# Second block of a two-block network: stages that end and begin by blocks of 128 tokens, with norms, transposes and router products block by block

## The chip, the cores and the metric

The kernel is written in Bass and runs on one core of one Trainium2 chip. The metric is the device time of one execution in microseconds. All data are float32. [...] A product (`mm`) of float32 shows as two records of MATMUL, each with a weight load of its own (LDWEIGHTS, on the row PEld); a transposition shows as one record.

## The reference, cut to what matters

x is 256 tokens by 1024 channels. Two networks follow each other, each of two layers. The first (attention and FFN) ends with an FFN of squared relus and an RMS norm:

```python
        ff = jnp.square(jax.nn.relu(jnp.einsum('bsd,df->bsf', h2, w_ff1[l])))
        x = x + jnp.einsum('bsf,fd->bsd', ff, w_ff2[l])
    return _rms_norm(x, final_g)
```

The second is modulated by a condition c:

```python
    for l in range(DEPTH):
        mod = cond @ ada_w[l] + ada_b[l]
        shift_m, scale_m, gate_m, shift_f, scale_f, gate_f = mods
        h = rms_norm(x, mix_norm_g[l]) * (1.0 + scale_m) + shift_m
        proj = h @ w_in[l]          # pooling, convolution and spatial gating parts
        ...
        x = x + gate_m * (mixed @ w_out[l])
        h = rms_norm(x, ffn_norm_g[l]) * (1.0 + scale_f) + shift_f
        # layer 0: y = swiglu(h), width 2816; layer 1: top 2 of 8 experts, width 3584
        x = x + gate_f * y
    return rms_norm(x, final_norm_g)
```

## The kernel before, in words

The engines' programs are written out by hand, in order, and meet at semaphores. The order of the work on an engine is the order of its program. x lies as [128 tokens, 2 blocks b, 1024]; hT is its normalised transpose, 8 tiles k of [128 channels, 256 tokens]. PSUM has eight banks: G0 to G3, T0, T1, S0, S1; H4 is the list S0, S1, T0, T1. A result of 256 tokens by 1024 columns fills the four G banks: bank j = 2*half + b holds columns of half `half` for the tokens of block b, and is called a quarter.

**Turn of a stage in the second block.** When a stage's last product is done, TensorE computes the gate sums (L2095, two products of 512 columns with a matrix of ones, into T1 and S1) and ScalarE copies them (L937) for a later gating. VectorE's `add_gated` waits for all four banks, multiplies each by the gate row (L1110) and adds it to x (L1114); ScalarE squares and sums block by block (L728); POOL's `norm_root` waits for both blocks and takes the root (L634, L635); VectorE scales both blocks (`normalise`, L1075); TensorE's `turn` waits for both, transposes them in four pairs into T0 and T1 (L1746), two tiles k over 256 tokens at a time, and ScalarE (L745) and VectorE (L1088) evacuate them with scale and shift into hT. Then TensorE starts the next stage. At the end of the first block there is a second norm in the chain: VectorE multiplies x by the final gain (L1443), ScalarE squares that too (L929), POOL takes two roots (L673 to L679) and L1446 scales by both.

**Mixer.** `features(0)`, `features(1)` (L2121, 24 products of 256 columns each) make the convolution's inputs, `tokens(2)` (L2113, 8 products of 256 columns for each block) the pooling's, `tokens(3)` and `tokens(4)` the gating unit's. VectorE makes the gated input, runs nine taps of the convolution (L1474, L1477) and then copies the two pooling banks (L1485, L1487), for which `tokens(3)` waits. At the end `product(k)` runs all four quarters for one tile k of the mixed channels; the last three tiles come from the convolution and are waited for one by one.

**FFN of layer 0.** Eleven steps of 256 hidden columns: `ffn_step` makes gate and up products (L2215, 4 x 8 products of 256 columns), then the down products of the step (L2221, 2 hidden tiles x 4 quarters of 512 columns) onto the G banks, which a product with zeros opens (L1756) and another closes (L1760). The weights lie in two slots of 3 MB that overlap the slots of the mixer's weights, so the second mixer's weights (L585) are asked for when both are free.

**Expert stage of layer 1.** Router products (L2233), selection, gather (L2247), then per expert 14 steps with five weight slots of 3 MB, filled from SyncE's queue (L573). POOL releases the first two slots behind `norm_root(U_FFN + 2)`, the other three behind the copies of the gate rows (L937).

**First block's FFN.** Eight chunks: up products in four tiles (L2047), ScalarE's relu (L918), VectorE's square (L1420), down products (L2054). The last chunk's second half of down products runs by quarters. In layer 1 ScalarE takes the sigmoid of the condition (L911) before the first relu; it waits for the condition and for the gate bias, which POOL asks for after the norm's root. VectorE and ScalarE do the modulation's products (`ada`, `row_sums`) between the chunks, with weights that POOL's queue brings (L651).

Of the kernel before, what the change touches and what calls it, by code (L numbers as in the profile page):

```python
# [9 lines left out]
ALU = mybir.AluOpType  # L10
# [3 lines left out]
P = 128  # L14
# [75 lines left out]
QUARTERS = ((0, 1, 2, 3), (0, 2, 1, 3))  # L90
ROW_L1 = 2 * KD + KCQ + KCKV
# [53 lines left out]
def build(nc, t):  # L145
    ctx = ExitStack()
    with ctx:
# [157 lines left out]
        rstd_ok = sig("rstd_ok", 1)  # L305
# [57 lines left out]
        w2_mm = sig("w2_mm", 7)  # L363
# [79 lines left out]
        def used_at(l, pos):  # L443

            return l * (L1_CHUNKS // NSLOT) + pos // NSLOT + 2

# [166 lines left out]
        def _(pool):  # L613
# [15 lines left out]
            def inv_root(v, out, count, u_wait, done):  # L629
# [5 lines left out]
                pool.tensor_tensor(out, v, mhalf[:, 0:n], ALU.pow).then_inc(done.sem, 1)  # L635

            def norm_root(u):
                pool.wait_ge(ss_ok.sem, ss_ok.at(u, 2))
                inv_root(small[:, 0:2], small[:, 2:4], None, u, rstd_ok)
# [13 lines left out]
            for l in range(DEPTH):  # L653
# [4 lines left out]
                inv_root(small[:, 8:28], small[:, 32:52], A_DIM, l, ars_ok)  # L658
# [6 lines left out]
                inv_root(small[:, 64:80], small[:, 80:96], 2 * B_DIM, l, subrs_ok)  # L665
# [6 lines left out]
            pool.wait_ge(ss_ok.sem, ss_ok.at(U_MIX, 2))  # L672
            step.do(pool.tensor_tensor(small[:, 0:2], small[:, 0:2], epsc[:, 0:2], ALU.add))  # L673
            step.do(pool.tensor_tensor(small[:, 2:4], small[:, 0:2], mhalf[:, 0:2], ALU.pow))
            step.do(pool.tensor_tensor(small[:, 6:8], small[:, 2:4], small[:, 2:4], ALU.mult))
            pool.wait_ge(ssq_ok.sem, 2)
            step.do(pool.tensor_tensor(small[:, 4:6], small[:, 4:6], small[:, 6:8], ALU.mult))
            step.do(pool.tensor_tensor(small[:, 4:6], small[:, 4:6], epsc[:, 0:2], ALU.add))
            pool.tensor_tensor(small[:, 304:306], small[:, 4:6], mhalf[:, 0:2], ALU.pow).then_inc(rstd_ok.sem, 1)  # L679
# [8 lines left out]
            for l in range(DEPTH):  # L688
                if l:
                    norm_root(U_MIX + 2 * l)  # L690
# [5 lines left out]
                norm_root(U_FFN + 2 * l)  # L696
# [21 lines left out]
        def _(act):  # L718
# [6 lines left out]
            def square_rows(u, b):  # L725

                act.wait_ge(x_new.sem, added(u, b))
                act.activation(squares[:, b, :], x[:, b, :], ACT.Square, scale=D ** -0.5, accum_out=small[:, b:b + 1]).then_inc(ss_ok.sem, 1)  # L728
# [44 lines left out]
            for l in range(DEPTH):  # L773
# [7 lines left out]
                act.wait_ge(rstd_ok.sem, rstd_ok.at(l * 2, 1))  # L781
# [127 lines left out]
                if l == DEPTH - 1:  # L909
                    act.wait_ge(ada_bias.sem, 32)  # L910
                    act.activation(condsig, condrow, ACT.Sigmoid).then_inc(cond_ok.sem, 1)  # L911
                for c in range(8):
# [6 lines left out]
                    if l == DEPTH - 1:  # L919
                        for n in ADA_SLOTS[0][c]:  # L920
                            row_sums(0, n)

            for l in range(DEPTH):
                u = U_MIX + 2 * l
                norm_squares(u)
                if l == 0:
                    for b in range(NB):
                        act.wait_ge(scaled_ok.sem, b + 1)
                        act.activation((pT, o)[b][:, :, :].rearrange("p i n -> p (i n)"), scaled[:, b, :], ACT.Square, scale=D ** -0.5, accum_out=small[:, 4 + b:5 + b]).then_inc(ssq_ok.sem, 1)  # L929
                def gate_rows(g):  # L930

                    for n, bank in ((1, T[1]), (0, S[1])):
# [5 lines left out]

                gate_rows(0)
                act.wait_ge(mulc_ok.sem, mulc_ok.at(l, 1))  # L940
                turned_evac(u, xn_turned, hT_act, mulc[:, l, 0], mods[:, l, 0:KD])

                for c in range(KCONV):
                    if c < 2:
                        act.wait_ge(w2_mm.sem, w2_mm.at(l, 3 + c))
# [24 lines left out]
                norm_squares(u + 1)  # L970
# [1556 lines left out]
```

## Time and profile before

| | |
|---|---|
| median of 3 runs | 2643.82 us (2643.2 to 2645.14) |
| profiled execution | 2643.71 us, its span 2641.7 us |
| granted TensorE clock, mean | 0.975 |
| TensorE busy | 2463.8 us, 93% |
| VectorE, ScalarE, POOL busy | 25%, 16%, 2% |
| DMA | 617.36 MB, mean 234 GB/s |

Busy matmul time is modelled and not a measure of peak; what counts here is where TensorE stands and what released it. In a timeline a row gives start, length, engine, line, operation, output<-input, shapes, count, and in brackets the idle time before it with its releaser.

### The profile page before, as it was taken

What the parts mean: (1) busy time and instruction counts of PE and PEld (TensorE: products, weight loads), DVE (VectorE), ACT (ScalarE), POOL (GpSimd) and SP (SyncE); (2) the same over time, 40 slices, a digit from 0 to 9 for tenths busy, and PEclk for the clock granted to TensorE, in tenths of its full rate; (3) what the DMA queues carried; (4) which work ended last, traced back from release to release, by engine and by line L of the source; (5) the groups of instructions that cost most, each with busy time, mean ns of one, the idle gap of its engine ahead of it and who ended that gap; (6) DMA issues with size and microseconds to landing.
All of it is one profiled execution on the core that took longest, in us unless ns stands there. A gap on an engine that the chain in (4) does not pass through costs nothing.

```text
span 2641.7 us, 27045 instructions
## 1 busy us (share of the span) xinstructions
PE 2463.8 (93%) x11010; PEld 1548.3 (59%) x11011; DVE 648.9 (25%) x1428; ACT 412.9 (16%) x1035; POOL 50.6 (2%) x96
## 2 busy tenths in 40 slices
PE   8999999999999999898998979888999889979997
PEld 5566566656664666656776744448984444434443
DVE  0453200013532244262343531111011101010101
ACT  1242000012430223101231010111001101000101
POOL 0000000000000000000000000000000000000000
PEclk9999999999999999999999989998998999999999
DMA  6323444333233777334774349995755999768971
GB/s 240 123 96 120 148 159 146 142 139 130 96 120 135 299 299 270 114 118 188 295 297 195 109 180 427 420 430 227 281 240 250 429 432 374 305 262 373 390 291 59
DMA packets 62540, 617.36 MB, mean 234 GB/s; under 512 B 4144, under 2 KB 4272, under 8 KB 36832
## 3 DMA queue, kind: packets, MB, share of 16 engines
q1 hardware_dynamic: 57488, 558.38, 52.9%
q0 software_dynamic: 4656, 56.47, 5.4%
q8 instruction: 89, 1.46, 0.2%
q10 hardware_dynamic: 288, 0.90, 0.1%
q14 instruction: 19, 0.16, 0.0%
HBM read 614.69 MB, written 1.05 MB: 233 GB/s over the span
## 4 chain that ended last, share of the span: by engine, by line
PE 82%; DMA 9%; DVE 3%; issue 3%; ACT 1%; POOL 1%; ACTq 0%; DVEq 0%; SPq 0%; POOLq 0%
DMA big<-in_moe_pack 9%; PE G L2054 8%; PE S L2280 7%; PE G L1781 6%; PE S L2278 5%; PE G L1819 5%; PE S L2047 4%; PE T L2047 4%; PE G L2293 4%; PE G L2001 3%; PE S L2215 3%; PE T L2215 3%; PE G L2221 3%; PE G L2291 2%; PE S L2344 2%
## 5 line engine op out<-in xcount | busy, mean ns | idle before, releaser
L2278 PE MATMUL S<-big,hT 128*64 128x256 f32 x2240 | 278.1, 392 | 67.0 <-DMA big<-in_moe_pack 41.2
L2278 PEld LDWEIGHTS S<-big,hT 128*64 128x64 f32 x2240 | 159.7, 140 | 182.8 <-issue 77.9
L2054 PE MATMUL G<-big 128*128 128x512 f32 x512 | 224.1, 596 | 6.3 <-DVE big L1420 6.3
L1654 DVE TENSOR_TENSOR probs<-S,probs 128x128 f32<-128x128 f32 (+2 forms) x105 | 35.5, 338 | 721.1 <-ACT probs L1008 721.1
L2280 PE MATMUL S<-big,hT 128*128 128x512 f32 x448 | 201.3, 593 | 1.3 <-issue 1.3
L1781 PE MATMUL G<-big,hT 128*128 128x372 f32 x512 | 162.1, 480 | 11.8 <-DMA big<-in_proj_pack 11.8
L1819 PE MATMUL G<-big,hT 128*128 128x384 f32 x512 | 171.0, 489 | 0.0
L2054 PEld LDWEIGHTS G<-big 128*128 128x128 f32 x512 | 98.0, 192 | 122.4 <-issue 121.6
L1781 PEld LDWEIGHTS G<-big,hT 128*128 128x128 f32 x512 | 98.2, 192 | 74.3 <-issue 13.2
L2291 PE MATMUL G<-big,pT 128*64 128x512 f32 x560 | 132.3, 593 | 8.3 <-ACT pT L1013 8.3
L2280 PEld LDWEIGHTS S<-big,hT 128*128 128x128 f32 x448 | 83.0, 190 | 95.6 <-issue 95.6
L1819 PEld LDWEIGHTS G<-big,hT 128*128 128x128 f32 x512 | 96.1, 190 | 65.1 <-issue 4.0
L2047 PE MATMUL T<-hT,big 128*128 128x256 f32 x512 | 113.5, 380 | 0.0
L2047 PE MATMUL S<-hT,big 128*128 128x256 f32 x512 | 113.5, 380 | 0.0
L1013 ACT ACTIVATE pT<-T 128x128 f32<-128x128 f32 (+1 forms) x98 | 30.2, 308 | 530.9 <-PE T L2264 530.9
L2047 PEld LDWEIGHTS S<-hT,big 128*128 128x128 f32 x512 | 97.5, 191 | 19.8 <-issue 7.6
L1420 DVE TENSOR_TENSOR big<-big 128x256 f32<-128x256 f32 x64 | 27.0, 425 | 320.9 <-ACT big L918 320.9
L2047 PEld LDWEIGHTS T<-hT,big 128*128 128x128 f32 x512 | 97.4, 190 | 12.9
L2293 PE MATMUL G<-big,pT 128*128 128x512 f32 x224 | 100.9, 594 | 3.3 <-ACT pT L1013 3.3
L2001 PE MATMUL G<-big,yT 128*128 128x512 f32 x192 | 83.1, 593 | 0.0
L2215 PE MATMUL S<-hT,big 128*128 128x256 f32 x352 | 81.4, 386 | 0.0
L2215 PE MATMUL T<-hT,big 128*128 128x256 f32 x352 | 79.6, 380 | 0.0
(356 smaller groups left out, 2727.8 us busy)
## 6 DMA issues: line engine op xcount, KB each, us to landing
big<-in_moe_pack SPq DMA_DIRECT2D x112, 3072.0 KB, 15.8
big<-in_w_ff SPq DMA_DIRECT2D x32, 2048.0 KB, 8.3
big<-in_ada_pack POOLq DMA_DIRECT2D x24, 2048.0 KB, 14.0
big<-in_ffn_pack SPq DMA_DIRECT2D x11, 3072.0 KB, 14.5
big<-in_gate_pack SPq DMA_DIRECT2D x16, 1536.0 KB, 6.2
big<-in_proj_pack SPq DMA_DIRECT2D x16, 1488.0 KB, 6.3
big<-in_branch_heads SPq DMA_DIRECT2D x6, 2048.0 KB, 7.7
big<-in_w_pack SPq DMA_DIRECT2D x8, 1536.0 KB, 6.2
```

Source lines behind the costliest of these rows:

```text
L1781: ins = mm(G[2 * (c % 2) + b][:, 0:PROJ_N], hT[:, k, b * P:(b + 1) * P], w[:, k, :], start=(k == 0), stop=(k == KD - 1))
L1819: ins = mm(G[b if n < 4 else 1][:, 0:GATE_N], hT[:, k, b * P:(b + 1) * P], w[:, k, :], start=(k == 0), stop=(k == KD - 1))
L2001: ins = mm(G[j][:, :], yT[:, 4 * n + k, b * P:(b + 1) * P], w[:, k, half * 512:(half + 1) * 512], start=(k == 0), stop=(k == 3))
L2047: ins = mm(H4[f][:, 0:SEQ], w[:, k, f * P:(f + 1) * P], hT[:, k, :], start=(k == 0), stop=(k == KD - 1))
L2054: return mm(G[j][:, :], hid[:, c % 2, f, b * P:(b + 1) * P], w[:, f, half * 512:(half + 1) * 512], start=(c == 0 and f == 0), stop=(c == 7 ...
L2215: ins = mm(H4[2 * f + piece][:, 0:SEQ], w[:, k, f * SEQ + piece * P:f * SEQ + (piece + 1) * P], hT[:, k, :], start=(k == 0), stop=(k == KD ...
L2221: ins = mm(G[2 * half + b][:, :], ffhid[:, i, f, b * P:(b + 1) * P], dn[:, f, half * 512:(half + 1) * 512], start=False, stop=False, skip_ ...
L2278: ins = mm(S[s % 2][f * FEW:(f + 1) * FEW, 0:SEQ], hTe[:, k, 0:FEW], wt[:, k, f * SEQ:(f + 1) * SEQ], start=(k == 0), stop=(k == KD - 1))
L2280: ins = mm(S[s % 2][:, :], hTe[:, k, 0:P], wt[:, k, :], start=(k == 0), stop=(k == KD - 1))
L2291: ins = mm(G[2][half * FEW:(half + 1) * FEW, :], ehid[:, s % 2, f * FEW:(f + 1) * FEW], wt[:, f, half * 512:(half + 1) * 512], start=first ...
L2293: ins = mm(G[2 + half][:, :], ehid[:, s % 2, f * P:(f + 1) * P], wt[:, f, half * 512:(half + 1) * 512], start=first, stop=last)
L2344: ins = mm(H4[2 * (s % 2) + piece][:, f * w:(f + 1) * w], wt[:, k, c0:c0 + P], hTe[:, k, 0:w], start=(k == 0), stop=(k == KD - 1))
```

## The change

The norms, transposes, and the first and last products of each stage of the second block are done by blocks of 128 tokens. `rstd_ok` now counts two per norm, `w2_mm` ten per layer. POOL's root, VectorE's `normalise` and both `turned_block` handle one block; `turn_block` transposes one block's eight tiles, four into each of two banks.

- At a turn TensorE transposes block 0, runs the gate sums (now into banks S1 and G1, or G0 and G2), and starts the next stage with products over block 0 only; block 1 is transposed between them. In the mixers `tokens_block(2, 0)` runs between block 1's transposes and its `features_block(0, 1)`.
- The stages before the turns end by quarters in the order `BY_ROWS` = 0, 2, 1, 3 (block 0 first): the mixer's last three tiles, the FFN's last two steps (both steps' gate and up products come before these downs), the first block's last chunk. VectorE's `gated_quarter` takes each as it comes.
- The first block's FFN in both layers runs the downs of chunk 6 after the ups of chunk 7, and all four tiles of chunk 7 by quarters.
- ScalarE's sigmoid of the condition moves behind the relus of chunk 0.
- The opening and closing products with zeros in the FFN are gone; the squares at the two turns out of the mixers go to an unused tile.

The core of the diff:

```diff
+BY_ROWS = QUARTERS[1]
...
+            def norm_root_by_rows(u):
+                for b in range(NB):
+                    pool.wait_ge(ss_ok.sem, ss_ok.at(u, b + 1))
+                    inv_root(small[:, b:b + 1], small[:, 2 + b:3 + b], None, rstd_ok)
...
-                if l == DEPTH - 1:
-                    act.wait_ge(ada_bias.sem, 32)
-                    act.activation(condsig, condrow, ACT.Sigmoid).then_inc(cond_ok.sem, 1)
                 for c in range(8):
...
                     if l == DEPTH - 1:
+                        if c == 0:
+                            act.wait_ge(ada_bias.sem, 32)
+                            act.activation(condsig, condrow, ACT.Sigmoid).then_inc(cond_ok.sem, 1)
...
+                act.wait_ge(mulc_ok.sem, mulc_ok.at(l, 2))
+                for b in range(NB):
+                    square_rows(u, b)
...
+                    turned_block(u, b, T[0], mulc[:, l, 0], mods[:, l, 0:KD])
                 gate_rows(0)
...
-                norm_squares(u + 1)
+                for b in range(NB):
+                    square_rows(u + 1, b)
+                    turned_block(u + 1, b, (T[0], G[1])[b], mulc[:, l, 1], mods[:, l, 3 * KD:4 * KD])
                 gate_rows(1)
...
+            def gated_quarter(j, g):
+                half, b = divmod(j, 2)
+                xs = x[:, b, half * 512:(half + 1) * 512]
+                step.do(dve.tensor_tensor(G[j][:, :], G[j][:, :], gateB[g][:, half * 512:(half + 1) * 512], ALU.mult))
+                dve.tensor_tensor(xs, xs, G[j][:, :], ALU.add).then_inc(x_new.sem, 1)
...
+                for i, j in enumerate(BY_ROWS):
+                    if i < 3:
+                        dve.wait_ge(w2_mm.sem, w2_mm.at(l, 8 + i))
+                    else:
+                        dve.wait_ge(used2(l, 8), used2_at(l, 8))
+                    gated_quarter(j, 0)
+                    if i == 2:
+                        normalise(u + 1, 0)
+                turned_block(u + 1, 0, T[1], mulc[:, l, 1], mods[:, l, 3 * KD:4 * KD])
+                normalise(u + 1, 1)
+                turned_block(u + 1, 1, G[3], mulc[:, l, 1], mods[:, l, 3 * KD:4 * KD])
...
+                    for d in (c,) if c < 6 else (6,) if c == 7 else ():
+                        weights(l, 25 + 2 * d)
+                        for f in range(4):
+                            pe.wait_ge(ff_ev.sem, ff_ev.at(l, 4 * d + f + 1))
+                            for j in range(4):
+                                ins = down_part(d, f, j)
...
-                    for f in (2, 3):
+                    for f in range(4):
                         ins = down_part(7, f, j)
...
-                features(0, (G[2], G[3], S[0]))
+                pe.wait_ge(xn_ok.sem, xn_ok.at(2 * l, 1))
+                turn_block(v, 0, T[0], T[1])
+                pe.wait_ge(x_new.sem, 4 * v + 3)
+                gate_sums(l, 0)
+                pe.wait_ge(hT_act.sem, hT_act.at(v, 1))
+                pe.wait_ge(hT_dve.sem, hT_dve.at(v, 1))
+                pe.wait_ge(x_new.sem, added(v))
+                features_block(0, 0, (G[2], G[3], S[0]))
+                pe.wait_ge(xn_ok.sem, xn_ok.at(2 * l, 2))
+                turn_block(v, 1, T[0], T[1])
+                tokens_block(2, 0, G[0])
+                pe.wait_ge(hT_act.sem, hT_act.at(v, 2))
+                pe.wait_ge(hT_dve.sem, hT_dve.at(v, 2))
+                features_block(0, 1, (G[2], G[3], S[0]))
+                pe.wait_ge(gateB_ok.sem, gateB_ok.at(l, 2))
                 features(1, (S[1], T[0], T[1]))
-                tokens(2, (G[0], G[1]))
+                tokens_block(2, 1, G[1])
...
+                pe.wait_ge(conv_ok.sem, conv_ok.at(l, 3))
+                for i, j in enumerate(BY_ROWS):
+                    half, b = divmod(j, 2)
+                    for k, pos, at in ((2, 7, 2), (3, 8, 0), (4, 8, 1)):
...
+                def up_step(n):
+                    pe.wait_ge(moe_in[(n + 1) % 2].sem, (n // 2 + 1) * 16)
+                    if n == 0:
+                        for piece in range(2):
+                            for f in range(FT):
+                                pe.wait_ge(fhid_ok.sem, f + 1)
+                                up_piece2(n, piece, f, 0, P)
+                            if piece == 0:
+                                second_block()
+                        second_ready()
...
+                    up_step(FSTEPS - 2)
+                    up_step(FSTEPS - 1)
+                    pe.wait_ge(fhid_ok.sem, (FSTEPS + 1) * FT)
+                    for i, j in enumerate(BY_ROWS):
+                        for n in (FSTEPS - 2, FSTEPS - 1):
+                            for f in range(FT):
+                                ins = down_piece(n, f, j)
...
+                    logits(0)
+                    second_block()
+                    second_ready()
+                    logits(1).then_inc(rt_mm.sem, 1)
+                    pe.wait_ge(gateB_ok.sem, gateB_ok.at(l, 4))
```

## Rows read from the trace of the kernel before

**Rows 1.** The page, part 4: the chain that ended last, by engine.

```profile
PE 82%; DMA 9%; DVE 3%; issue 3%; ACT 1%; POOL 1%; ACTq 0%; DVEq 0%; SPq 0%; POOLq 0%
```

**Rows 2.** Timeline: start and duration in us, engine, line, operation, count, idle before.

```profile
873.32 1.06 ACT L911 ACTIVATE big<-big 128x1024 f32<-128x1024 f32 x1 [11.86 <-DMA big<-in_gate_bias]
875.32 15.51 PE L2054 MATMUL G<-big 128*128 128x512 f32 x32 [6.27 <-DVE big L1420]
...
1069.76 13.90 PE L2054 MATMUL G<-big 128*128 128x512 f32 x32
```

**Rows 3.** Timeline at A, TensorE, and VectorE's copy of the pooling bank.

```profile
1083.49 1.02 PE L2095 MATMUL T<-big,misc 128*128 128x512 f32 x2
...
1096.35 9.08 PE L2121 MATMUL G<-hT,big 128*128 128x256 f32 x32 [1.14 <-ACT hT L745]
...
1119.09 7.07 PE L2113 MATMUL G<-big,hT 128*128 128x256 f32 x32
1126.67 20.91 PE L2113 MATMUL G<-big,hT 128*128 128x384 f32 x64 [0.52 <-DVE big L1487]
...
1123.51 0.42 DVE L1485 COPY big<-G 128x256 f32<-128x256 f32 x1
```

**Rows 4.** Timeline at B, TensorE.

```profile
1193.42 1.02 PE L2095 MATMUL T<-big,misc 128*128 128x512 f32 x2
...
1208.63 5.39 PE L2215 MATMUL S<-hT,big 128*128 128x256 f32 x16
...
1224.21 7.03 PE L2221 MATMUL G<-big,pT 128*128 128x512 f32 x16
```

**Rows 5.** Timeline at C, TensorE.

```profile
1437.88 0.95 PE L1760 MATMUL G<-zcol,vecs 128*128 128x2 f32 x8
...
1473.96 7.07 PE L2113 MATMUL G<-big,hT 128*128 128x256 f32 x32
```

**Rows 6.** Timeline: the chain inside B; last, POOL's first add at A.

```profile
1193.68 1.30 DVE L1110 TENSOR_TENSOR G<-G,diag 128x512 f32<-128x512 f32 x2 [10.61 <-issue]
...
1198.86 1.06 ACT L728 ACTIVATE yT<-x 128x1024 f32<-128x1024 f32 x1 [1.38 <-DVE x L1114]
...
1200.09 0.20 POOL L634 TENSOR_TENSOR small<-small,epsc 128x2 f32<-128x2 f32 x1 [23.24 <-ACT yT L728]
...
1201.09 1.42 DVE L1075 TENSOR_SCALAR rot<-x,small 128x1024 f32<-128x1024 f32 x2 [2.26 <-POOL small L635]
...
1085.71 1.05 POOL L673 TENSOR_TENSOR small<-small,epsc 128x2 f32<-128x2 f32 x1 [58.92 <-ACT yT L728]
```

**Rows 7.** Timeline elsewhere: transposes, evacuations and products of 128 columns.

```profile
541.83 1.04 PE L1769 MATMUL T<-vecs,x 128*128 128x128 f32 x8
...
1582.54 1.37 DVE L1637 TENSOR_SCALAR hT<-G,misc,mods 128x128 f32<-128x128 f32 x4 [6.62 <-PE G L2247]
1582.60 1.50 ACT L995 ACTIVATE hT<-G,mods,misc 128x128 f32<-128x128 f32 x4 [13.52 <-PE G L2247]
...
1669.60 3.84 PE L2247 MATMUL G<-yT,rot 128*128 128x128 f32 x32
...
1159.28 1.61 PE L2162 MATMUL G<-big 128*128 128x128 f32 x12
...
1576.07 6.43 PE L2247 MATMUL G<-yT,rot 128*128 128x128 f32 x32 [1.64 <-DVE yT L1630]
```

**Rows 8.** DMA: loads issued at 1396, at 1438.1; timeline, the expert stream and D's E.

```profile
big<-in_ffn_pack SPq DMA_DIRECT2D x1, 3072.0 KB, 9.9
...
big<-in_w_pack SPq DMA_DIRECT2D x1, 1536.0 KB, 6.1
...
1555.41 44.80 SPq L573 DMA_DIRECT2D big<-in_moe_pack  x7
...
1548.30 1.02 PE L2095 MATMUL T<-big,misc 128*128 128x512 f32 x2
```

**Rows 9.** Windows of 2 us: busy us of each engine (instructions), granted clock, DMA share, GB/s.

```profile
1198.00:1200.00 2.00, 0.00 (x0) 0.00 (x0) 0.83 (x2) 1.14 (x3) 0.00 (x0) 0.82 1.03 442
```

More of the change, by code:

```diff
@@ L627, in _, with inv_root @@
             pool.wait_ge(half_ok.sem, 1)
-            def inv_root(v, out, count, u_wait, done):
+            def inv_root(v, out, count, done, by=1):
                 n = v.shape[1]
@@ L727, in square_rows, with turned_block @@
                 act.wait_ge(x_new.sem, added(u, b))
-                act.activation(squares[:, b, :], x[:, b, :], ACT.Square, scale=D ** -0.5, accum_out=small[:, b:b + 1]).then_inc(ss_ok.sem, 1)
+                act.activation(squares[:, b, :] if u not in BETWEEN else unused, x[:, b, :], ACT.Square, scale=D ** -0.5, accum_out=small[:, b:b + 1]).then_inc(ss_ok.sem, 1)
+            def turned_block(u, b, bank, mul, add):
+                act.wait_ge(xn_turned.sem, xn_turned.at(u, 2 * b + 1))
+                for k in range(KH):
+                    ins = act.activation(hT[:, k, b * P:(b + 1) * P], bank[:, k * P:(k + 1) * P], ACT.Identity, scale=mul[:, k:k + 1], bias=add[:, k:k + 1])
+                ins.then_inc(hT_act.sem, 1)
             def norm_squares(u):
@@ L924, in _ @@
                 u = U_MIX + 2 * l
[L925 to L929, printed above, removed]
                 def gate_rows(g):
-                    for n, bank in ((1, T[1]), (0, S[1])):
+                    for n, bank in gate_banks(g):
                         act.wait_ge(gateB_mm.sem, gateB_mm.at(l, 2 * g + 2 - n))
@@ L2206, in ffn_step @@
[L2206 to L2209 removed]
+                arrived(8)
+                pe.wait_ge(conv_ok.sem, conv_ok.at(l, 3))
+                for i, j in enumerate(BY_ROWS):
+                    half, b = divmod(j, 2)
+                    for k, pos, at in ((2, 7, 2), (3, 8, 0), (4, 8, 1)):
+                        w = slot(chunk2(l, pos))[:, at * D + half * 512:at * D + (half + 1) * 512]
+                        ins = mm(G[j][:, :], mixT[:, k, b * P:(b + 1) * P], w, start=False, stop=(k == OUT_ORDER[-1]))
+                        if i == 3 and k == 2:
+                            ins.then_inc(used2(l, 7), 1)
+                    ins.then_inc(w2_mm.sem if i < 3 else used2(l, 8), 1)
@@ new lines, in up_piece2 @@
+                def up_piece2(n, piece, f, c0, c1):
+                    w = moe_slot((n + 1) % 2)[0]
+                    for k in range(KD):
+                        ins = mm(H4[2 * f + piece][:, c0:c1], w[:, k, f * SEQ + piece * P:f * SEQ + (piece + 1) * P], hT[:, k, c0:c1], start=(k == 0), stop=(k == KD - 1))
+                    return ins
+                def up_step(n):
[8 more added lines that the diff above has]
+                        second_ready()
@@ L2222, in ffn_step, with down_piece @@
-                    ins.then_inc(moe_free[place].sem, 1)
-                if l == 0:
-                    open_banks()
-                    for n in range(FSTEPS):
-                        ffn_step(n, n % 2, (n + 1) % 2, n // 2 + 1)
-                    close_banks(fdn_done)
+                            up_piece2(n, piece, f, P if n == 0 else 0, SEQ).then_inc((fg_mm, fu_mm)[piece].sem, 1)
+                def down_piece(n, f, j):
+                    half, b = divmod(j, 2)
+                    dn = moe_slot((n + 1) % 2)[1]
+                    return mm(G[j][:, :], ffhid[:, n % 2, f, b * P:(b + 1) * P], dn[:, f, half * 512:(half + 1) * 512],
+                              start=(n == 0 and f == 0), stop=(n == FSTEPS - 1 and f == FT - 1))
```

230 lines of the change are left out of this document (117 added, 113 removed).

## The prediction

> **What bounds the kernel now.** I read the page's chain first: most of the end is set by TensorE [rows 1]. So only stretches in which TensorE stands, or runs at the lower clock, can give time back, and I read its timeline at each place that the diff touches, then the other engines inside those gaps. Call A, B, C, D the four turns of the second block's stages: into its first mixer, first FFN, second mixer, expert stage; E is the moment when TensorE's last product before the turn ends. A fifth place, Z, is the start of the first block's second FFN.
>
> At Z ScalarE waits 11.86 us at L911 for the gate bias (the sigmoid of the condition); the relus are queued behind it, so TensorE stands 6.27 us and its next 32 products take 15.51 us, where the same 32 take 13.90 elsewhere [rows 2]. At A the first product (L2121) starts at 1096.35, 12.86 us after E = 1083.49, and its first 32 run 9.08 us, against 7.07 for the same shape later [rows 3]. At B: 15.21 us from E = 1193.42 to 1208.63 [rows 4]. At C E = 1437.88 [rows 5]. Inside such a gap the reader sees one chain (B): multiply, add, square, root, scaling, transposes, evacuation, each for all 256 tokens before the next begins [rows 6].
>
> **Z.** The sigmoid moves behind the first four relus. TensorE's stall goes and with it the slow products: 6.27 + (15.51 - 13.90) = **7.9 us**. What is late next: the ada products on VectorE, which need the sigmoid only after the next chunk (ups and downs, 2 x 13.7 us on); the bias has landed by 873.32 [rows 2]. Nothing.
>
> **Order at the stage ends.** Each bank's last products are now together, the two banks of block 0 first. The count is the same. At A and C a quarter is 4 products of 512 columns, 8 records, 3.43 us (13.90 us hold 32 records at a pitch of 0.429 [rows 2]); at B and D 3 products, 2.57 us. Block 0 is complete at E - 6.9 (A, C) or E - 5.1 (B, D).
>
> Block 0's chain at B, by durations of [rows 6]: the bank is seen 0.26 us after its end (1193.42 to 1193.68), one multiply 0.70 (two took 1.30) and its add over the same 512 columns 0.70, ready at E - 3.5; square with its read 1.2 (1198.86 to 1200.09), E - 2.3; roots 1.0 (to 1201.09), E - 1.3. VectorE meanwhile takes the third quarter (E - 2.6 + 0.26 + 1.4 = E - 0.9), then scales block 0 in 0.71: E - 0.2. So the transposes start at E, without a gap. At A the chain has the second norm in it (two squares, six root steps), but 6.9 us to hide in; at C 6.9 us too. 8 transposes take 1.04 us [rows 7]; the gate sums (two products, 4 records at 0.43, 1.72 us) now fill TensorE behind them, to E + 2.8. Evacuation: ScalarE four in 1.50, VectorE four in 1.37 [rows 7], but VectorE first takes the fourth quarter, to E + 1.7, so it ends at E + 3.05 at B, C, D; at A, where a quarter is one operation, the gate sums end last. First product: E + 2.8 at A, **E + 3.15 at B and D**.
>
> **The price of halves.** A product over 128 tokens needs the same two weight loads. 32 records of 128 columns took 3.84 us [rows 7], pitch 0.118, against 0.216 for 256 columns (7.07 us for 32 [rows 3]). So each of 320 records (96 at A, 128 at B, 96 at C) costs 0.010 more than half a wide one: 3.2 us, contained below. Bounds: no premium (0.108), and 0.134, from 12 records in 1.61 us [rows 7]: 5.1 us dearer than my 0.118. I take 0.118, the row with most records.
>
> **A.** Products of block 0 (48 x 0.118 = 5.7) to E + 8.5; block 1's norm chain ends about E + 7.0, covered; transposes 1.04; the pooling product of block 0, moved up as cover, 3.46; block 1's 5.7; the second chunk 10.4: E + 29.0, against 1119.09 - 1083.49 = 35.6 before [rows 3]: 6.6 us. Then only half the pooling product (3.46 us) covers VectorE, which takes conv taps ahead of the copy that frees the banks, until 1123.51 [rows 3]; two copies, 0.42 each, and 0.1: 5.4 us after the chunk's end, so TensorE stalls 1.9 us where it stalled 0.52. Before, that point was 7.58 us after the chunk's end (1126.67 [rows 3]). **A = 6.6 + 2.2 = 8.8 us.**
>
> **B.** 3.8 (piece 0, block 0) + 1.04 (transposes) + 3.8 + 7.6 (second halves) from E + 3.15: first down product at E + 19.3, against 1224.21 - 1193.42 = 30.8 [rows 4]. Block 1's scaled rows are there at E + 5.1, before TensorE asks at E + 6.9. **11.5 us**, the lower clock at its start (5.39 for 16 [rows 4], 3.6 at full clock) and the bank opening included. The ada loads start behind gate rows that come some 3 us later; nothing reads them for two steps, 40 us.
>
> **End of the FFN.** The ups of the last two steps run together, then all downs by quarters, behind a wait for the last hidden tile. No product covers VectorE's last multiply: 0.26 + 0.42 = **0.7 us lost**. The last step's weights are now asked for one set of ups (64 records at 0.216, 13.8 us) before use, not ups and downs (20.7); such a load landed in 9.9 us [rows 8]: 0.
>
> **C.** The weights of the second mixer can only be asked for when the FFN's slots are free, at E + 0.2, and the first chunk landed 6.1 us later [rows 8]. Before, the 15 us gap hid that; now it is what comes last: first product at E + 6.3. TensorE stands from 2.8 to 6.3. After that as at A: 6.3 + 5.7 + 1.04 + 3.46 + 5.7 + 10.4 = E + 32.6, against 1473.96 - 1437.88 = 36.1 [rows 5]: 3.5, and the 2.2 of the copies: **5.7 us**. Does the clock fall in these 3.5 us? [...] I take no fall; the other end is 2.0 us, as at A.
>
> **D.** Experts' weights stream without a gap from 1555.41 [rows 8] and experts 0 and 1 wait for them, so what counts is the stream's start, not TensorE. POOL releases it behind the norm's root: 7.1 us after E = 1548.30 [rows 8]. Now the square of block 1 is queued on ScalarE behind block 0's evacuation: E + 2.1 + 1.2 + 0.5 for the root's issue = E + 3.8. **3.3 us.** TensorE's own gain (some 9 us to the logits) only lengthens its wait for weights; the slots 2 to 4 wait for gate rows at about E + 9.8, while the first two loads last until E + 18.
>
> **Sum**: 7.9 + 8.8 + 11.5 - 0.7 + 5.7 + 3.3 = 36.5 us. The profiled execution took 2643.71 us (span 2641.7 and 2.0 around it), 0.1 from the median of the runs, 2643.82: **2607.2 us**. The first block's quarters (doubled in size) cost nothing: TensorE has the same products, and its other work between them is in place.
>
> [...] One small add on POOL took 1.05 us while VectorE ran a product of two SBUF operands; the same took 0.20 when VectorE stood [rows 6]. The new order puts POOL's steps beside VectorE's work. Worked out from the rows: 0.85 at B moves block 0's scaling from E - 0.2 to about E + 0.3, and the fourth quarter comes last anyway; at A and C the slack is over a microsecond. I take 0, at most 0.5 a turn, 2 in all. [...]
>
> **Rivals.**
> 1. *The block chain comes late.* If block 0's rows are ready 3 us after E (VectorE's in-order queue: its scaling stands behind a quarter; POOL's steps slow), A, B and D lose 3 us each; C is covered by the weights. With the clock falling at C: 2607 + 9 + 2 = **2618**. For: chains slip by more than a row's sum. Against: only 3.15 us at B rest on it, and each row repeats at four turns.
> 2. *More comes back*: halves at 0.108, and the slots freed earlier for expert weights closing a gap in the stream: 2607 - 3 - 1 to 2: **2602**.
> [...]
> 4. *It does nothing where it matters*: waits of the last products (for all three conv tiles) or a late first load eat the turns, only Z is left: **2636**.
>
> **Chances.** Forecast (2603 to 2612) 0.62; rival 1 (2612 to 2622) 0.18; rival 2 (under 2603) 0.12; rival 3 0.03; rival 4 0.05. The range 2600 to 2620 holds the forecast, most of rival 1 and half of rival 2, about 0.8. Within 0.2% is 5.3 us, about what a measurement of this kernel can tell from no change. Faster: all of 1, 2, 4 and the forecast, less mishaps, 0.95; same 0.02; slower 0.03.
>
> **What the profile after would show.** Right: no TensorE wait at Z; transposes starting within 0.3 us of E; first products at E + 2.8, 3.15, 6.3 (the last released by a weight DMA); a stall of about 1.9 us ahead of the third mixer product; 128-column records at 0.118; the expert stream starting 3.8 us after E. Wrong: a transposition waiting on VectorE for microseconds, a granted clock of 0.5 at a turn, or a new stall inside the mixers or at the FFN's end.

## The result and the profile after

The changed kernel took 2611.34 us (median, 2610.02 to 2613.76), the kernel before 2644.11 beside it: ratio 0.9877, interval 0.986 to 0.9894, 32.8 us less. The forecast was 2607.2 us, from a sum of 36.5 us. The profiled execution took 2613.76 us with a span of 2611.7, 30.0 less than the span of before.

The page of the kernel after: its first part, and the chain by engine; TensorE's share is up from 82% [rows 1].

```profile
PE 2453.1 (94%) x11154; PEld 1541.9 (59%) x11155; DVE 652.7 (25%) x1444; ACT 416.8 (16%) x1051; POOL 52.6 (2%) x108
...
PE 84%; DMA 10%; DVE 2%; issue 2%; ACT 1%; POOL 0%; ACTq 0%; DVEq 0%; SPq 0%; POOLq 0%
```

Timeline of TensorE after, at Z and A (the places of [rows 2, 3]): no wait in the line of Z; at A the transposes start in the moment when the products end, then come the gate sums, then the first products, 2.60 us behind E. Counts such as x32 are records, two for each product.

```profile
870.21 13.90 PE L2077 MATMUL G<-big 128*128 128x512 f32 x32
...
1076.77 1.04 PE L2133 MATMUL T<-vecs,rot 128*128 128x128 f32 x8
1077.65 1.02 PE L2119 MATMUL S<-big,misc 128*128 128x512 f32 x2
1078.51 1.02 PE L2119 MATMUL G<-big,misc 128*128 128x512 f32 x2
1079.37 3.76 PE L2152 MATMUL G<-hT,big 128*128 128x128 f32 x32
1082.96 1.95 PE L2152 MATMUL S<-hT,big 128*128 128x128 f32 x16
...
1110.03 20.91 PE L2140 MATMUL G<-big,hT 128*128 128x384 f32 x64 [1.61 <-DVE big L1524]
```

The same at B [rows 4] and C [rows 5], and the queue of SP with the first expert weights at D [rows 8]; E of D is 1515.20.

```profile
1176.95 1.04 PE L2133 MATMUL T<-vecs,rot 128*128 128x128 f32 x8
...
1179.96 2.02 PE L2279 MATMUL S<-hT,big 128*128 128x128 f32 x16 [0.25 <-issue]
...
1409.65 1.04 PE L2133 MATMUL T<-vecs,rot 128*128 128x128 f32 x8
...
1415.94 5.44 PE L2152 MATMUL G<-hT,big 128*128 128x128 f32 x32 [3.54 <-DMA big<-in_w_pack]
...
1448.28 20.91 PE L2140 MATMUL G<-big,hT 128*128 128x384 f32 x64 [1.61 <-DVE big L1524]
...
1518.90 7.29 SPq L581 DMA_DIRECT2D big<-in_moe_pack  x5
```

From E to the first point where both kernels do the same work again, before and after: A 43.18 and 33.26 (the first product of `tokens(3)`, in the lines of 128x384; the expectations below call it the fourth pool product), B 30.79 and 18.25 (first down product), C 43.67 and 38.63, D 7.11 and 3.70 (stream). With Z (8.0), the FFN's end (-0.8) and 0.3 lost inside the two mixers that is 37.8 us; the sum forecast 36.5. But the spans differ by 30.0 only. 1.3 us of the rest had gone before the first edit is reached: the second FFN of the first block begins at 855.52, at 854.20 before. Executions scatter there: over the runs below that have Z's stall removed, the first down products of that FFN start anywhere from 868.9 to 872.4. The other 6.5 us went behind all edits. The gather behind expert 0 starts 36.9 us earlier than before, the one behind expert 1 36.0, the one behind expert 2 30.9, and the span ends 30.0 earlier. This is the chain of waits where expert 2 begins, of the kernel before:

```profile
1785.69 5.15 issue
1790.84 4.21 PE G L2247 x19
1795.05 0.93 issue
1795.98 2.76 PE G L2247 x13
```

and of the kernel after:

```profile
1749.68 11.13 issue
1760.81 6.99 PE G L2352 x32
```

"Issue" is time in which an engine waits for nothing that the profile shows. TensorE stands for 5.15 and 0.93 us in the one, where its gather stops once behind 19 records, and for 11.13 in the other, where the 32 records of the gather follow without a stop. Nobody touched this code.

### The profile page after: what moved, and what is told of

It reads as the page before. It is cut to its first block, busy times and chain, and to the rows that moved or that the text cites. A ratio compares the mean times of both kernels' runs of the same rounds, so it can differ in the third digit from the quotient of the medians.

```text
span 2611.7 us, 27388 instructions
## 1 busy us (share of the span) xinstructions
PE 2453.1 (94%) x11154; PEld 1541.9 (59%) x11155; DVE 652.7 (25%) x1444; ACT 416.8 (16%) x1051; POOL 52.6 (2%) x108
## 3 DMA queue, kind: packets, MB, share of 16 engines
q8 instruction: 90, 1.47, 0.2%
HBM read 614.69 MB, written 1.05 MB: 236 GB/s over the span
## 4 chain that ended last, share of the span: by engine, by line
PE 84%; DMA 10%; DVE 2%; issue 2%; ACT 1%; POOL 0%; ACTq 0%; DVEq 0%; SPq 0%; POOLq 0%
DMA big<-in_moe_pack 9%; PE G L2077 8%; PE S L2385 7%; PE G L1804 6%; PE S L2383 6%; PE G L1842 5%; PE S L2070 4%; PE T L2070 4%; PE G L2398 4%; PE G L2024 3%; PE S L2279 3%; PE T L2279 3%; PE G L2302 3%; PE G L2396 2%; PE S L2449 2%; PE G L2036 2%
## 5 line engine op out<-in xcount | busy, mean ns | idle before, releaser
L2070 PE MATMUL T<-hT,big 128*128 128x256 f32 x512 | 113.4, 379 | 0.0
L2070 PE MATMUL S<-hT,big 128*128 128x256 f32 x512 | 113.4, 379 | 0.0
L2279 PE MATMUL S<-hT,big 128*128 128x256 f32 (+1 forms) x384 | 80.2, 362 | 0.2 <-issue 0.2
L2279 PE MATMUL T<-hT,big 128*128 128x256 f32 (+1 forms) x384 | 80.1, 362 | 0.0
```

The costliest lines, as they stand in the source:

```text
L2070: ins = mm(H4[f][:, 0:SEQ], w[:, k, f * P:(f + 1) * P], hT[:, k, :], start=(k == 0), stop=(k == KD - 1))
L2279: ins = mm(H4[2 * f + piece][:, c0:c1], w[:, k, f * SEQ + piece * P:f * SEQ + (piece + 1) * P], hT[:, k, c0:c1], start=(k == 0), stop=(k = ...
```

## The experiments

Twelve kernels in three groups; each group shared its runs of the kernel before. The changed kernel's own second measurement is the yardstick, and since the executions of one kernel lie 1.4 to 7.9 us apart, what decides is mostly a stretch of the trace. Over the kernels that leave them alone A and B repeat within 0.1 us, C within 0.3.

| run | median us | before | ratio, interval |
|---|---|---|---|
| changed, again | 2612.35 | 2644.37 | 0.9881 (0.9866 to 0.9896) |
| z_alone | 2633.32 | 2644.37 | 0.9965 (0.9951 to 0.9978) |
| d_release | 2608.99 | 2644.37 | 0.9868 (0.9853 to 0.9883) |
| c_fill | 2605.10 | 2644.37 | 0.9854 (0.9839 to 0.9869) |
| pad20 | 2610.10 | 2645.60 | 0.9862 (0.9845 to 0.9879) |
| pad4 | 2605.54 | 2645.60 | 0.9848 (0.9831 to 0.9864) |
| copy_first | 2609.23 | 2645.60 | 0.9858 (0.9841 to 0.9874) |
| b_whole | 2617.07 | 2645.60 | 0.9889 (0.9873 to 0.9906) |
| best4 | 2594.73 | 2644.62 | 0.9813 (0.9799 to 0.9826) |
| d_whole | 2613.34 | 2644.62 | 0.9883 (0.9867 to 0.9898) |
| a_short | 2612.97 | 2644.62 | 0.9879 (0.9864 to 0.9894) |
| unhoist | 2617.70 | 2644.62 | 0.9894 (0.9879 to 0.9909) |

**The changed kernel again.** 

> The changed kernel once more, nothing edited. Time: 2610 to 2614 us. The question is the 6 us that the first execution gave back in the expert stage: of the 37 us by which expert 1 begins earlier, 31 are left when expert 3 begins. Theory (the gap comes with the layout of the program): the critical chain shows again about 11 us of issue near 1750 us, where the kernel before has 5. Rival (the gap is chance of one execution): it is 5 us here, and the span is about 6 us shorter.

The piece is 11.43 us at 1748.49, so it belongs to the program, not to chance.

**The sigmoid alone (z_alone)**, in the kernel before:

```
-  if l == DEPTH - 1:
-      act.wait_ge(ada_bias.sem, 32)
-      act.activation(condsig, condrow, ACT.Sigmoid).then_inc(cond_ok.sem, 1)
   ...
+  if c == 0:
+      act.wait_ge(ada_bias.sem, 32)
+      act.activation(condsig, condrow, ACT.Sigmoid).then_inc(cond_ok.sem, 1)
```

> The kernel before with one thing of the change: ScalarE takes the sigmoid of the condition behind the first relus instead of ahead of them. Theory (the terms add up, each where it was priced): 7.9 us less than the kernel before, 2636.2 us; the products into the first mixer norm start about 8 us earlier, and every stage behind keeps its length. Rival (half of what is gained ahead is given back in the expert stage, as the trace of the changed kernel suggests with its 6 us): 2 to 6 us less only, and the issue gap between two experts is longer than in the kernel before.

11 us less by the medians, but with an interval from 5.8 to 13.0 us, which holds 7.9 too; the trace decides. TensorE reaches A's gate sums 8.0 us earlier (1075.50 instead of 1083.49), as priced. Another 1.9 us is in the first products behind them, which follow the same idle times with another duration (timeline of z_alone; before, the last line took 9.08 us [rows 3]):

```profile
1083.01 1.94 PE L1746 MATMUL T<-vecs,rot 128*128 128x128 f32 x8 [5.62 <-DVE rot L1446]
1085.27 1.81 PE L1746 MATMUL T<-vecs,rot 128*128 128x128 f32 x8 [0.32 <-ACT hT L745]
1088.22 7.14 PE L2121 MATMUL G<-hT,big 128*128 128x256 f32 x32 [1.14 <-ACT hT L745]
```

The windows of 10.5 and 10 us from A's gate sums on have a granted clock (1.00 is full speed) of 0.81 and 0.69 before, 0.71 and 0.96 here. After the same waits the granted clock was higher, and the 32 records took 1.9 us less. Why it did, no run here settles. The first gather of the expert stage starts 10.1 us earlier. The issue piece at expert 2 is 4.46 and 1.79 us, as before, with TensorE's program untouched: the rival (half of the gain is given back) is out for this part of the change.

**The expert slots released earlier (d_release).**

```
+  for b in range(NB):
+      pool.wait_ge(ss_ok.sem, ss_ok.at(U_FFN + 2 * l, b + 1))
+      inv_root(small[:, b:b + 1], small[:, 2 + b:3 + b], None, rstd_ok)
+      if b == 0:
+          for pos in (8, 7):
+              pool.wait_ge(used2(l, pos), used2_at(l, pos))
+          for i in range(2):
+              pool.sem_inc(moe_free[i].sem, 1)
```

> The changed kernel with the two first expert weight slots given free by GpSimd between the root of block 0 and that of block 1 of the last norm, where it gave them free behind both. Theory (what starts the first expert's weight stream sets the stage): the stream starts at the end of the last down product +0.3 us instead of +3.7, and the kernel is 3.4 us shorter, 2608 us. Rival (the router's chain of products, top-k and gathers sets it): the stream starts as early, and the time is within 0.5 us of the changed kernel's.

The stream starts 0.42 us behind E instead of 3.70, the gather of expert 0 no earlier (19.35 us behind E in both), and the gather at that expert's end 3.2 us earlier, counted from E. From the stream's start to that gather it is 113.75 us after and 113.85 here: the stream sets this stage.

**The hole at C filled (c_fill).** SP loads the chunk of pool step 2 first, into a free slot, and at the second mixer:

```
-  features_block(0, 0, (G[2], G[3], S[0]))
+  tokens_block(2, 0, G[0])
   pe.wait_ge(xn_ok.sem, xn_ok.at(2 * l, 2))
   turn_block(v, 1, T[0], T[1])
-  tokens_block(2, 0, G[0])
+  features_block(0, 0, (G[2], G[3], S[0]))
```

> The changed kernel with the weights of one pool step of the second mixer loaded ahead, into a slot that is free, and TensorE's order at the start of that mixer turned to pool product, turning of block 1, first feature product. Theory (the hole of 3.54 us in which TensorE waits for a weight load costs its own length and a fall of the clock): 3.5 us for the wait and 1.7 us for the 32 products that took 5.44 us instead of 3.73, in sum 5 us less, 2606 us, and no product group of 5.4 us there. Rival 1 (what follows, VectorE's taps and the gated inputs, is what the stage waits for): the wait of the fourth pool product grows from 1.6 to about 5 us and the time stays within 1 us. Rival 2 (the clock falls all the same): 3.5 us less.

From E to `tokens(3)` it takes 33.71 us instead of 38.63: 4.9 less, and the wait ahead of it is still 1.61, so rival 1 is out. Timeline of c_fill; no wait for a DMA is left, and the 32 records take 3.73 us at a granted clock of 1.00 (5.44 at 0.69 in the changed kernel), so rival 2 is out:

```profile
1411.59 3.69 PE L2138 MATMUL G<-big,hT 128*128 128x256 f32 x16 [0.24 <-issue]
1415.12 1.04 PE L2131 MATMUL T<-vecs,rot 128*128 128x128 f32 x8
1415.99 3.73 PE L2150 MATMUL G<-hT,big 128*128 128x128 f32 x32
```

**The program shifted (pad20, pad4).** With 20, or 4, for N:

```
+  for _ in range(N):
+      mm(G[0][:, 0:2], ident[:], zcol[:], start=True, stop=True)
   pe.wait_ge(chosen_ok.sem, 1)
```

> The changed kernel with 20 products of two columns more on TensorE, ahead of the router's rank products, where TensorE sits idle for 4.3 us. They are there to move every instruction behind them by 40 places (a product is two instructions, weight load and multiply). [...]
The pieces in the chain, of pad4 and then of pad20:

```profile
1748.39 5.59 issue
```

```profile
1751.31 5.22 issue
```

Both halved it, pad4 too, against its expectation. pad4 reaches the wide gather 17.95 us behind the one before it, the changed kernel 23.49 and 23.80: 5.5 to 5.9 us less. The medians are 6.8 apart (2612.35 to 2605.54, from different groups). Four products do nothing for the computation and make the kernel faster. What comes in during the wait shows in the DMA queues, page part 3 for a window around the piece. Columns are packets, MB, share. First the changed kernel (1748 to 1761), then pad4 (1747 to 1754):

```profile
q8 instruction: 2, 0.03, 1.0%
```

```profile
q8 instruction: 1, 0.02, 1.0%
```

Two packets of the instruction queue within the wait (one between 1750 and 1754, one between 1758 and 1762), against one. So it is in all fourteen traces, counted over the piece: one packet in five pieces (z_alone 4.46 us, best4 4.79, before 5.15, pad20 5.22, pad4 5.59), two in nine (c_fill 9.82, unhoist 10.43, a_short 10.45, d_whole 10.71, copy_first 11.09, after 11.13, d_release 11.35, after2 11.43, b_whole 11.74). The queue of the expert weights (q1) has a share of 97 to 109% in these windows; all queues together have 1.01 from 1749.7 to 1760.8 in the changed kernel. Over the whole execution the pages of the five count 89 such packets, those of the nine 90, but b_whole's 91. By the page a packet has some 16 KB (90 packets, 1.47 MB). From 1647 to 1751 us the changed kernel has none at all: there expert 1 runs the code that expert 0 ran, while expert 2, the only wide one, is the first to run its own.

That TensorE waits there for its own program is my reading: the profile counts the packets and does not say which engine's instructions they bring, nor how long one takes. What the runs show is what a few instructions more ahead of the experts do to the piece. A float32 product is four instructions of TensorE, two weight loads and two multiplies, as the records show (pad4's page has 11162 and 11163 where the changed kernel's has 11154 and 11155, for 4 products); the expectations above counted two. The changed kernel has 288 such records more than the kernel before, and the piece is 11.13 us instead of 5.15. pad4 adds 16 to them, pad20 80, and it is 5.59 and 5.22. The one instruction more that d_whole (below) was expected to have leaves it at 10.71, and b_whole's 128 records less leave it at 11.74. The three with a pad (pad4, pad20, best4) have the shorter piece, the changed kernel and its other variants the longer; where the border lies no run shows. The kernel before stops once more, for 0.93 us behind 19 of the 32 records of its wide gather, with one packet between 1792 and 1796; z_alone stops behind the same record, for 1.79 us, with one between 1782 and 1786. In the changed kernel, pad4, pad20 and best4 the 32 records follow each other without a stop, in 6.99 us.

Two things stay open. In b_whole one more packet comes just ahead of the wait (between 1752 and 1754), beside the two within it (between 1756.16 and 1758, and between 1764 and 1768); in no other trace is there one in the 6 us ahead, and what it brings isn't shown. And a wait with one packet isn't always 4.5 to 5.6 us: where expert 1 begins, every kernel, the one before too, has a piece of 6.0 to 7.6 us with one packet.

pad20 has the shorter piece too, but its 20 products took 8.67 us, 0.43 each, at a granted clock of 0.50: they delay the router by 4.1 us (first gather 23.4 us behind E). All of that is absorbed by expert 0's end (113.84 us from the stream's start, as always): the router has that much slack. Its profiled execution is 3.0 us behind pad4's already at Z, where nothing differs. Over the four executions of each, its span is 1.0 us longer in the median (2604.6 and 2603.6). The rest of the 4.6 us between the medians lies outside the span, where pad20 has 5.2 to 5.5 us and pad4 1.8 to 3.0; why stays open.

**VectorE's copy first (copy_first).**

```
+  dve.wait_ge(w2_mm.sem, w2_mm.at(l, 1))
+  dve.tensor_copy(poolA[:, 0, :], G[0][:, 0:POOL_W]).then_inc(pool_ev.sem, 1)
   ...
-  conv_taps(9)
-  dve.wait_ge(w2_mm.sem, w2_mm.at(l, 1))
-  dve.tensor_copy(poolA[:, 0, :], G[0][:, 0:POOL_W]).then_inc(pool_ev.sem, 1)
+  conv_taps(6)
```

> The changed kernel with VectorE's order at the start of both mixers turned: the copy of the first pool bank ahead of the gated inputs, and six taps between it and the second copy instead of nine. Theory (the 1.61 us for which TensorE waits ahead of the fourth pool product in each mixer are on the path): the wait falls to about 0.5 us in each layer and the kernel takes 2.2 us less, 2609 us. Rival (the three taps and the copy only change places, and what waits for the taps at the end of the conv is late instead): the wait is gone and the time is the same within 0.5 us.

The line of `tokens(3)` in copy_first, A:

```profile
1111.04 4.14 PE L2140 MATMUL G<-big,hT 128*128 128x384 f32 x12 [0.52 <-DVE big L1524]
```

0.52 instead of 1.61, and the same at C: A is 32.16 us (33.26), C 37.69 (38.63), and from there to the mixer's end it is 66.92 us in all. 2.0 us, where 2.2 were expected; nothing behind got late.

**The first FFN's step whole (b_whole).**

```
-  for piece in range(2):
-      for f in range(FT):
-          up_piece2(n, piece, f, 0, P)
-      if piece == 0:
-          second_block()
+  second_block()
   ...
-  up_piece2(n, piece, f, P if n == 0 else 0, SEQ)
+  up_piece2(n, piece, f, 0, SEQ)
```

> The changed kernel with the first feed-forward step of both layers in the old manner: both blocks are turned first, then the 32 products run over 256 columns at once. Theory (at this stage the split saves what it takes to scale, turn and evacuate the second block): the first product starts 6.7 us behind the end of the mixer instead of 3.0, and the kernel takes 3.7 us more, 2615 us. Rival (ScalarE's and VectorE's own chain behind the products, silu and product, sets when the first down product can run): 1 us more or less.

B is 24.04 us instead of 18.24, so 5.8 more; the rival's 1 us did not come. Timeline of b_whole:

```profile
1183.31 1.47 PE L2133 MATMUL G<-vecs,rot 128*128 128x128 f32 x8 [2.26 <-DVE rot L1098]
1186.29 5.84 PE L2279 MATMUL S<-hT,big 128*128 128x256 f32 x16 [1.51 <-ACT hT L750]
1191.97 3.62 PE L2279 MATMUL T<-hT,big 128*128 128x256 f32 x16
```

3.6 us are the waits, 2.2 the clock: 16 records in 5.84, at a granted clock of 0.62, that take 3.62 one line later, at 1.00. The theory had the first and left out the second.

**All together (best4).** The edits of d_release, c_fill, copy_first and pad4.

> The changed kernel with what four of the earlier runs showed to pay, together: the early release of the two expert slots, the weights of a pool step loaded ahead with TensorE's order for it, the copy of the pool bank ahead of the gated inputs, and the 4 products that shift the program by 8 places. Theory (the parts lie one behind the other and add up): 3.1 + 4.9 + 2.0 + 5.7 = 15.7 us less than the changed kernel, 2596 us. Rival (the earlier stream meets the router's chain, which is then late: only 3.7 us of slack were there): the first expert's stage is up to 1 us longer, 2597 us and more.

2594.73 us, 49.9 less than before and 17.6 less than the changed kernel (15.7 expected, medians of different groups). From E: A 32.16, C 32.62, stream at 0.42, expert 0's end 114.33 behind E (117.45 in the changed kernel), the piece:

```profile
1737.64 4.79 issue
```

The rival did not come: 114.33 - 0.42 is 113.9, the length that the stream always had.

**The router whole (d_whole).**

```
-  logits(0)
   second_block()
   second_ready()
+  logits(0)
```

> The changed kernel with the router's products of block 0 behind the evacuation of block 1, as in the kernel before. Theory (the expert weight stream sets the first expert's stage, and the router's chain has about 4 us of slack, as the run with 20 products showed): the first gather is up to 1 us later, the second one is not, and the time is the changed kernel's. Rival (the block by block order of the router earns part of the 3.4 us): 1 us slower behind the first expert. One instruction more also shifts the program by one place: the issue piece at expert 2 stays at 11 us if the threshold lies beyond it, and falls to 5.5 if not.

The first gather starts 22.83 us behind E (19.35 in the changed kernel), the gather at expert 0's end 117.42 (117.45). The block by block order of the router gives TensorE 3.5 us, and none of it counts. The piece is 10.71 us: the one instruction more does not shorten it.

**Less cover at the FFN's end (a_short).**

```
-  for d in (c,) if c < 6 else (6,) if c == 7 else ():
+  for d in (c,):
-      for f in range(4):
+      for f in range(4 if c < 7 else 2):
```

> The changed kernel with the first block's feed-forward ending as in the kernel before: the last whole down quarter runs in its old place, and the last step is halved, so that block 0 is complete only 3.4 us ahead of TensorE's last product. Theory (what covers block 0's chain is the product time behind its last addition): the chain of block 0 is late at both places where a mixer of the second block or the first block's own last norm begins, the first products into the first mixer start about 2 us later, 2613.5 us. Rival (the chain has enough cover even so): the time is the changed kernel's within 0.5 us.

Timeline of a_short at A; the transposes wait, as they do nowhere in the changed kernel:

```profile
1080.72 1.10 PE L2133 MATMUL T<-vecs,rot 128*128 128x128 f32 x8 [1.94 <-DVE rot L1181]
```

That and a slower transpose are 2.1 us from the FFN's first down product to `tokens(3)`; the medians (2612.97 and 2612.35, different groups) cannot show it. So doubling the quarters, which I had costed at nothing, is also what covers the chain at A. At the other place, the first layer's last norm, the transposes (545.00) follow the products without a wait; that half of the expectation failed.

**The pooling product back (unhoist).** `tokens_block(2, 0, G[0])` again behind the features of block 1.

> The changed kernel with the pool product of step 2 back in its place behind the features of block 1, in both mixers. Theory (it covers the evacuation of block 1's turned columns, 1.5 us, but takes that much cover from VectorE's first copy): 1.5 us of wait appear ahead of block 1's features at each mixer and 1.1 us go at the fourth pool product, so 0.8 us more in sum, 2612 us. Rival (only the first half holds): 3 us more.

Timeline of unhoist at A:

```profile
1086.46 3.81 PE L2152 MATMUL G<-hT,big 128*128 128x128 f32 x32 [1.51 <-ACT hT L750]
...
1111.27 7.04 PE L2140 MATMUL G<-big,hT 128*128 128x384 f32 x21 [1.94 <-DVE big L1524]
```

1.5 us of wait appear as priced, but the one ahead of `tokens(3)` grows from 1.61 to 1.94. A is 2.1 us longer, C too, and at C the 64 records behind the longer wait took 22.60 us instead of 20.91, with a granted clock of 0.66 in their first 5 us: 5.9 us in all, 5.3 by the medians. The full product of 7 us did not give the cover back, but this run cannot say that it never would. ScalarE's sigmoids wait for counts of `w2_mm`, which the pooling product also raises, and the edit left these counts as they were. With the product moved, each of the first two sigmoids waits for one result more than it needs. ScalarE in unhoist, released by the pooling product (L2140), and in the changed kernel, released by its own features (L2161):

```profile
1105.91 0.66 ACT L971 ACTIVATE big<-T 128x256 f32<-128x256 f32 x2 [6.52 <-PE G L2140]
```

```profile
1101.55 0.38 ACT L971 ACTIVATE big<-T 128x256 f32<-128x256 f32 x1 [3.07 <-PE T L2161]
1105.00 0.38 ACT L971 ACTIVATE big<-T 128x256 f32<-128x256 f32 x1 [3.07 <-PE T L2161]
```

So the last gated input starts 30.7 us behind E (28.7 in the changed kernel), and VectorE's copies stand behind it and nine taps. What the order alone costs stays open; the wait of 1.5 us ahead of the features comes before these counts play a part.

## Why the prediction was right

The time is inside the range and 4.1 us over the forecast. The mechanism came as described at all six places, but for the clock at C; that the total came so near is partly luck, as told below. By its steps:

- **Z** 7.9: 8.0. In the kernel alone it brings 1.9 more at A, by the clock; in the changed kernel that part is inside A, since A was read against the slow products of before [rows 3].
- **A** 8.8: 9.9. First product at E + 2.60 (forecast 2.8), stall 1.61 (1.9). Block 0 was scaled by E - 1.4: the six root steps had cover, and a_short shows that they need it.
- **The price of halves** was mis-sized: 32 records of 128 columns take 3.59 us from start to start (1079.37 to 1082.96), 0.112 each, between my bound of 0.108 and the 0.118 that I took from the expert gather. Over 320 records that is 1.9 us to my favour, 1.3 of it at A and B, which together gave 2.1 over their terms.
- **B** 11.5: 12.5, first product at E + 3.01 (3.15). b_whole shows 5.8 of it to be the split of this one step, 2.2 of them clock.
- **End of the FFN** 0.7 lost: 0.78, 0.52 of it in the wait for the last hidden tile. **D** 3.3: 3.41, and d_release, pad20 and d_whole show why: the stream sets expert 0.
- **C** 5.7: 5.0. First product at E + 6.29, on a weight load, as forecast. "I take no fall" failed: behind the wait of 3.54 us the 32 records there took 5.44 us at a granted clock of 0.69, at A 3.76 at 1.00. That is 1.7 us, inside the other end of 2.0. To take none was my estimate: at B before, the mean was 0.82 from 1198 to 1200, with TensorE idle [rows 9], and at which length of wait the clock falls no run shows. From the first product to the end of the second chunk A took 25.4 us where 26.3 were forecast; as much at C hid about half of the fall.
- **POOL beside VectorE**: 0 was right, but not because there is nothing of what [rows 6] show. Before, POOL's add of 1.05 us ended at 1086.76, with VectorE's product of two SBUF operands (1084.36 to 1086.71). After, at A, block 0's add came when that product was over and took 0.18; block 1's met it, took 0.37 and ended with it again, at 1080.40 and 1080.35. A product for one block is shorter and was nearly done. At B, C and D the adds took 0.18 or 0.19. What couples the two no run tests; block 1's add took 0.19 us more than block 0's.

VectorE before, then VectorE and GpSimd after, at A:

```profile
1084.36 2.35 DVE L1443 TENSOR_TENSOR probs<-x,yT 128x1024 f32<-128x1024 f32 x2
```

```profile
1079.13 1.22 DVE L1176 TENSOR_TENSOR probs<-x,yT 128x1024 f32<-128x1024 f32 x1
...
1072.19 0.18 POOL L689 TENSOR_TENSOR small<-small,epsc 128x1 f32<-128x1 f32 x1 [52.11 <-ACT yT L744]
...
1080.03 0.37 POOL L689 TENSOR_TENSOR small<-small,epsc 128x1 f32<-128x1 f32 x1 [5.49 <-ACT yT L744]
```

What no step had: that stages behind the last edit would keep their length. The sum ended at D, and the 5.7 us by which the piece at expert 2 grew lay outside it. That is larger than any error of a term. It is also more than the 3.7 us by which the sum was too hopeful, since the terms themselves gave 1.3 more than forecast: 37.8 - 5.7 is 32.1, and the medians gave 32.8. The range was wide enough for a loss that nothing in the prediction names. Of the rivals none came whole: no chain was late, the short products ran at a granted clock of 1.00 at A and B (3.76 us for 32 records at A, 2.02 for 16 at B), and all four turns gave something; of rival 2 the cheaper halves came in part.

## What to carry to other kernels

Price a turn between stages from the row that ends last in it, and sum; it held within 1.1 us at each of six places. Add, as the far end of a range, what the next products may lose to the clock behind a wait of TensorE. Here it was 1.7 us behind 3.54 us (C), 2.2 behind 2.26 and 1.51 us (b_whole), 1.7 behind 1.94 us at C of unhoist, and nothing behind the same 1.94 us at A of unhoist and of a_short. Where a kernel branches into long bodies, compare the chain's issue pieces at the jumps before and after. Here the piece at expert 2 was 11.13 us where the kernel before had 5.15, and four idle products in a wait ahead of the experts brought it to 5.59. And when a product is moved in a hand-written order, renumber the counts that wait for its neighbours.

## What was not expected of the hardware

- Where expert 2 begins TensorE stands for 4.46 to 5.59 us with one packet of the instruction queue in the wait (five traces) and for 9.82 to 11.74 with two (nine), beside a queue of expert weights with a share of 97 to 109%; where expert 1 begins it is 6.03 to 7.62 with one, at 96 to 103%. 16 records of TensorE more (pad4) took it from 11.13 to 5.59.
- The same waits at the same place (5.62, 0.32, 1.14 us) were followed by 32 records in 9.08 us in one kernel and 7.14 in another that reaches them 8 us earlier.
- A product of 2 columns takes 0.43 us ahead of the experts (40 records in 8.67 us in pad20, at a granted clock of 0.50), as much as the router's of 8 columns (1536.77 to 1537.20 in the same trace). Four of 2 columns at the FFN's end took 0.81 us from start to start before, 0.20 each, at a granted clock of 1.00 [rows 5]. Small products are not free, only hidden.
- The first 870 us of the program scatter by 3.5 us from execution to execution. From there to D the five traces whose code is the same there differ by 0.2 us. The stage of expert 1 scatters by 1.8 again (103.1 to 104.9). So single medians a few us apart say less than one stretch of the trace.
